# Sums of squares on TensorE between the products, behind four norms of a two-block network

## The reference

```python
def rmsnorm(x, g):
    y = xf * lax.rsqrt(jnp.mean(xf * xf, axis=-1, keepdims=True) + NORM_EPS)
    return (y * g.astype(jnp.float32)).astype(x.dtype)
# first block, for layer i
    a = rmsnorm(h, norm_mix_pre[i])
    m = mla_mixer(a, ...) if i % 2 == 0 else pool_mixer(a, ...)
    h = h + rmsnorm(m, norm_mix_post[i])
    f = conv_ffn(rmsnorm(h, norm_ffn_pre[i]), ...)
    h = h + rmsnorm(f, norm_ffn_post[i])
# second block
    u = _rmsnorm(h, ln1_g[i]); proj = u @ w_in[i]
```

## Time and profile before

| | |
|---|---|
| median of 3 runs | 948.71 us (945.36 to 949.46) |
| profiled execution | 950.01 us, span 948.2 us |
| mean granted TensorE clock | 0.984 |
| busy: TensorE, VectorE, ScalarE, GpSimd | 96%, 72%, 54%, 29% |
| first products of f0, a1, f1, g start at | 142.7, 354.5, 387.7, 592.2 us |

### The profile page before, as it was taken

The page is one execution under the profiler, slowest core; times in us unless marked ns, Lnnn a source line. Parts: engine busy times, 40 slices in busy tenths (PEclk is TensorE's granted clock), DMA queues, the critical chain, the costliest instruction groups (busy, mean ns, idle before and its releaser), DMA issues.

```text
span 948.2 us, 19994 instructions
## 1 busy us (share of the span) xinstructions
PE 912.0 (96%) x7354; PEld 884.7 (93%) x7354; DVE 681.7 (72%) x1168; ACT 512.9 (54%) x851; POOL 276.4 (29%) x202
## 2 busy tenths in 40 slices
PE   6999999999999999999999999999989999999996
PEld 6986798999999997899999999999989999999995
DVE  7767529999994225699999533889777888785666
ACT  5765656666655346566666544454455554454443
POOL 4118752000015534200000464200024334345633
PEclk9999999999999998799999999999999999999997
DMA  7541132544554531144445554354234555465431
GB/s 249 181 158 46 46 134 89 178 177 177 177 196 164 210 133 46 45 177 177 177 177 210 184 188 174 96 194 157 89 113 174 185 201 182 177 227 184 166 134 45
DMA packets 22147, 146.80 MB, mean 155 GB/s; under 512 B 2752, under 2 KB 5328, under 8 KB 6736
## 3 DMA queue, kind: packets, MB, share of 16 engines
q1 hardware_dynamic: 22096, 146.11, 43.1%
HBM read 143.94 MB, written 1.05 MB: 153 GB/s over the span
## 4 chain that ended last, share of the span: by engine, by line
PE 83%; DVE 10%; ACT 3%; issue 2%; POOL 1%; DMA 0%; POOLq 0%; SPq 0%; DVEq 0%; ACTq 0%
PE bank L441 23%; PE bank L442 23%; PE bank L443 23%; PE bank L681 2%; DVE u_low L1332 2%; ACT w_high L959 1%; DVE w_low L1323 1%; PE bank L529 1%; DVE h L1405 1%; PE bank L814 1%; DVE bank L1397 1%; PE bank L697 1%; PE bank L543 1%; PE bank L715 1%; PE bank L512 1%
## 5 line engine op out<-in xcount | busy, mean ns | idle before, releaser
L441 PE MATMUL bank<-u_high,w_high 128*128 128x256 f32 (+2 forms) x1400 | 401.7, 287 | 13.1 <-DVE u_low L1332 8.6
L442 PE MATMUL bank<-u_low,w_high 128*128 128x256 f32 (+2 forms) x1400 | 399.4, 285 | 0.0
L443 PE MATMUL bank<-u_high,w_low 128*128 128x256 f32 (+2 forms) x1400 | 398.2, 284 | 0.0
L1832 POOL TENSOR_TENSOR w_low<-raw,w_high 128x512 fp32r<-128x512 f32 (+1 forms) x60 | 168.8, 2814 | 463.0 <-ACT w_high L959 463.0
L1323 DVE TENSOR_TENSOR w_low<-raw,w_high 128x1024 fp32r<-128x1024 f32 (+5 forms) x119 | 198.1, 1664 | 125.7 <-ACT w_high L959 124.6
L441 PEld LDWEIGHTS bank<-u_high,w_high 128*128 128x128 f32 x1400 | 266.1, 190 | 15.5 <-DVE u_low L1332 8.1
L442 PEld LDWEIGHTS bank<-u_low,w_high 128*128 128x128 f32 x1400 | 265.8, 190 | 0.0
L443 PEld LDWEIGHTS bank<-u_high,w_low 128*128 128x128 f32 x1400 | 265.5, 190 | 0.0
L959 ACT ACTIVATE w_high<-raw 128x1024 fp32r<-128x1024 f32 (+5 forms) x119 | 195.2, 1640 | 73.2 <-PE bank L443 65.0
L441 PE MATMUL bank<-x_high,w_high 128*128 128x256 f32 (+1 forms) x608 | 173.9, 286 | 4.4 <-ACT x_high L1261 2.5
L443 PE MATMUL bank<-x_high,w_low 128*128 128x256 f32 (+1 forms) x608 | 173.3, 285 | 0.0
(11 more groups left out here) (213 smaller groups left out, 1030.1 us busy)
## 6 DMA issues: line engine op xcount, KB each, us to landing
raw<-w_up_dram SPq DMA_DIRECT2D x66, 1024.0 KB, 4.8
raw<-w_down_dram SPq DMA_DIRECT2D x24, 1408.0 KB, 6.1
raw<-w_gin_c_dram SPq DMA_DIRECT2D x4, 1536.0 KB, 6.8
raw<-w_wo_dram SPq DMA_DIRECT2D x4, 1024.0 KB, 5.0
raw<-w_wout_dram SPq DMA_DIRECT2D x4, 1024.0 KB, 4.9
raw<-w_pgate_dram SPq DMA_DIRECT2D x4, 1024.0 KB, 4.7
raw<-w_gin_v_dram SPq DMA_DIRECT2D x2, 1024.0 KB, 4.7
raw<-w_gin_g_dram SPq DMA_DIRECT2D x2, 1024.0 KB, 6.2
```

The lines of the kernel that those rows point to most:

```text
L441: nc.tensor.matmul(out, hi, rhi, start=start, stop=False)
L442: nc.tensor.matmul(out, hi, rlo, start=False, stop=False)
L443: return nc.tensor.matmul(out, lo, rhi, start=False, stop=stop)
L1832: nc.gpsimd.tensor_tensor(wl[n % 2][:, at], raw[n % 2][:, at], wh[n % 2][:, at].bitcast(F32), ALU.subtract).then_inc(low_parts_g, pool_cou ...
```

## The change

- In the first unit of f0, f1 and g TensorE takes the sums of chunk k - 1 over m between chunk k's products with u_high and those with u_low; behind the unit only chunk 7's sums are left. The eps product moves to the first of these.
- In a1 the sums of chunks 0 to 2 stand between the first tile's products of the first half, those of 3 to 7 in a row between the halves.
- GpSimd no longer adds squares or clears `acc` for these four norms.
- In `add_post` (all four places) the scaled chunk is written back to m, and the addition reads it there.

```diff
@@ unit
+                        if sums is not None and k > 0:
+                            sums(k - 1)
                         low_ready(k)
...
+            def sums_by_chunks(name, n):
+                def of(k):
+                    if k == 0:
+                        nc.tensor.matmul(bank[NORM_BANK][:, 0:n], eps_w[:, :], ones[:, 0:n], start=True, stop=False,
+                                         skip_group_check=True)
+                    chunk_sums(name, n, k)
+                return of
...
@@ ffn_up
-                unit(n0, T, us, high_then_low(sums_name))
-                norm_sums(sums_name, f"{sums_name} acc {DC - 2}", squares(0, T), True)
+                n = len(squares(0, T))
+                if l < 2:
+                    unit(n0, T, us, high_then_low(sums_name), sums=sums_by_chunks(sums_name, n))
+                    last_sums(sums_name, n)
+                else:
+                    unit(n0, T, us, high_then_low(sums_name))
+                    norm_sums(sums_name, f"{sums_name} acc {DC - 2}", squares(0, T), True)
...
@@ a1
+                                if half == 0 and 2 * g + k > 0:
+                                    sums(2 * g + k - 1)
                                 low_ready(2 * g + k)
...
                 if half == 0:
-                    norm_sums("a1", f"a1 acc {DC - 2}", squares(0, T1), True)
+                    for k in range(DC // 2 - 1, DC - 1):
+                        sums(k)
+                    last_sums("a1", len(TT))
...
@@ g
-            unit(n, T, us, high_then_low("g"))
-            norm_sums("g", f"g acc {DC - 2}", squares(0, T), True)
+            unit(n, T, us, high_then_low("g"), sums=sums_by_chunks("g", len(squares(0, T))))
+            last_sums("g", len(squares(0, T)))
...
@@ add_post
-                spare = 3 * (unit % 2) + 2
-                normed = bank[NORM_BANK][:, 64:64 + Tm], bank[spare][:, 0:Tm]
...
-                    nc.vector.tensor_tensor(normed[c % 2], m[:, c, 0:Tm], bank[R_BANK][:, 0:Tm], ALU.mult)\
+                    nc.vector.tensor_tensor(m[:, c, 0:Tm], m[:, c, 0:Tm], bank[R_BANK][:, 0:Tm], ALU.mult)\
...
-                        nc.vector.tensor_tensor(h[:, c, T1 - Tm:T1], h[:, c, T1 - Tm:T1], normed[c % 2], ALU.add)\
+                        nc.vector.tensor_tensor(h[:, c, T1 - Tm:T1], h[:, c, T1 - Tm:T1], m[:, c, 0:Tm], ALU.add)\
...
@@ add_square on GpSimd
-                if name in SQUARES_IN_M:
-                    pool.wait_ge(*done(f"{name} u low {c}"))
...
@@ GpSimd, the same for a1, f1 and g
-            for c in range(DC - 1):
-                add_square("f0", c, T1, done(f"f0 sq {c}"))
             up_lows(0)
-            clear("f0")
```

More of the change, by code:

```diff
@@ L446, in weights, with unit @@
                 return wh[n % 2][:, j * P:(j + 1) * P], wl[n % 2][:, j * P:(j + 1) * P]
-            def unit(n, T, xs, chunk_ready=None, middle=None, i=None, order=None, first_low=None, between={}):
+            def unit(n, T, xs, chunk_ready=None, middle=None, i=None, order=None, first_low=None, between={}, sums=None):
                 U = UNITS[n]
@@ L785, in _ @@
             parts_ready(n)
+            sums = sums_by_chunks("a1", len(TT))
             for half in range(2):
@@ L1892, in _ @@
             clear("post0")
-            for c in range(DC - 1):
-                add_square("f0", c, T1, done(f"f0 sq {c}"))
             up_lows(0)
-            clear("f0")
             down(0, T1)
             clear("fpost0")
-            for c in range(DC - 1):
-                add_square("a1", c, T1, done(f"a1 sq {c}"))
-            clear("a1")
             for b in range(DC - 2):
@@ L1905, in _ @@
             clear("post1")
-            for c in range(DC - 1):
-                add_square("f1", c, SEQ + HISTORY, done(f"f1 sq {c}"))
             up_lows(1)
-            clear("f1")
             down(1, SEQ)
@@ L1912, in _ @@
             clear("fpost1")
-            for c in range(DC - 1):
-                add_square("g", c, T, done(f"g sq {c}"))
             for n in range(FIRST_UNIT["gin_a"] + 2, FIRST_UNIT["gin_c"] + 6):
                 low(n)
-            clear("g")
             for u in range(4):
```

## The result

The changed kernel takes 952.74 us (median of 20 executions, 948.74 to 959.76) against 949.19 us of the kernel before beside it (20 executions, 944.39 to 952.36): ratio 1.0037, 95% interval 1.0022 to 1.0052. It is a little slower, by about 0.4%. The prediction was 952.9 us. The profiled execution took 953.30 us, its span is 951.5 us.

A forecast was written before the change was run, and what follows sets the result against it. TensorE was taken to bound the kernel, VectorE to pace f0's first unit. 0.56 + 0.90 + 0.93 + 1.78 - 1.7 + 1.7 = +4.2 us, from the runs' median 948.71 us to 952.9 us; range 948.5 to 959.0 us.

The forecast's parts named there:

- each chunk's sums cost 0.67 us: First units of f0, f1, g: 0.67 us of sums (g 0.45) exceed the 0.41 us wait, so TensorE becomes the bound.
- The term for it without cover: VectorE's longer addition from m: at most 2.2 us over four norms if TensorE's 0.22 us surplus per chunk didn't hide it.
- The low part of the next unit: VectorE, behind f0's first unit: ends at about 153.7 instead of 154.3 us, so TensorE's wait for it goes.
- Its own term, +1.78 us: a1: chunks 3 to 7's sums in a row, 3.35 us, replace 1.57 us of eps and sums between the halves.
- I count one more such stretch: +1.7 us: a1: the row of sums brings one more low-clock stretch, sized like the one behind f1, +1.7 us.
- 3.35 us with nothing but one-column sums: a1: reason given for the added low clock; the row is longer than the tail that cost f1 its clock.
- I count -1.7 us: Behind f1: the new tail has no wait and one chunk of sums, so the low clock there goes, -1.7 us.
- rival (c): Clock gives more back: f0's and f1's tails fall often before, never after, a1 loses none; +0.8 us, 949.5 us, chance 0.11.
- (a): Clock falls inside the first units: 954.6 to 960 us in f0 or f1 alone, up to 967 in both; chance 0.28.
- (b): Sums hide in the waits if a chunk's six passes take at most 0.41 us: -3.3 us, 945.4 us; chance 0.07.
- (d): A later wait absorbs the delay of the sums: +0, 948.7 us; chance 0.04.
- The chance of 0.44: Whole kernel slower by over 0.5% (above 953.5 us): 0.17 from the main forecast plus 0.27 from (a).

The follow-up runs named there:

- e6: The changed kernel without the sums of chunks 0 to 6 in f0, f1 and g (left out altogether): 947.45 us against 947.95, ratio 0.9991.
- e2: The kernel before with only the scaled block written to m, all sums still on GpSimd: 949.58 us against 948.49, ratio 1.0021.
- e1: The changed kernel with the scaled block going to PSUM again, so only the sums move to TensorE: 953.27 us against 948.49, ratio 1.0050.
- e4: The changed kernel with squares written as fp32r into x_high and summed in one pass instead of two: 939.78 us against 948.49, ratio 0.9928.
- e3: The changed kernel with a1's sums on GpSimd and over acc again: 949.15 us against 948.49, ratio 1.0025.
- e8: The changed kernel with f0, f1 and g back on GpSimd, only a1 with the new sums: 953.93 us against 947.95, ratio 1.0063.
- e5: The changed kernel with a1's sums of chunks 3 to 6 spread between second and third token tile's products: 954.62 us against 947.95, ratio 1.0060.
- e7: The one-pass kernel e4 with a1's sums of chunks 3 to 6 spread as in e5: 942.59 us against 947.95, ratio 0.9927.
- e10: The one-pass kernel e4 with 32 equal columns for each sum instead of 2: 943.53 us against 948.35, ratio 0.9955.
- e11: The changed kernel without a1's sums of chunks 0 to 6 (left out altogether): 947.18 us against 948.35, ratio 1.0000.
- e12: The one-pass kernel e4 measured once more, unedited, against the kernel before: 942.77 us against 948.02, ratio 0.9939.
- e9: The changed kernel with each sum of f0, a1, f1 and g written to 32 equal columns: 952.26 us against 948.35, ratio 1.0033.

## Why the prediction was right

**What bounds the first units.** Right, to the hundredth. The chunk was worked out as 0.75 + 0.67 = 1.42 us and is 1.42 us; e6 shows that without the passes it is 1.11 us. f0: +0.59 measured, +0.56 predicted. f1: +0.82 against +0.90. g: +1.00 against +0.93. In g's six later chunks the step from sums to sums is 1.51 us, predicted 1.50. The step "each chunk's sums cost 0.67 us" (0.45 in g) held.

**VectorE.** Right that the move to m would be hidden. The term for it without cover (at most 2.2 us) had the right size by luck: e2, without cover, pays 2.1 us, hardly by a longer addition (0.35 us in a steady chunk) but by a u_low that takes 0.59 us beside GpSimd, and the accumulation 0.85. It came out at nothing for the reason that GpSimd has left, and not only by TensorE's surplus: VectorE's chunk is 1.11 us with the block in PSUM (e1) and with the block in m, and in e4 it is so where VectorE sets the pace again. The low part of the next unit was predicted to end at 153.7 us; it ends at 152.65, since it takes 2.28 us and not 2.85 without GpSimd's last accumulation beside its start. The step took its length from the earlier trace rows unchanged. It had no effect, since TensorE's sums end later.

**a1.** Its own term, +1.78 us, held, and two more were off. By the loads, the first half without its last row takes 10.36 us (354.58 to 364.94; before 354.50 to 364.52, 10.02): +0.34 us for eps and the sums of chunks 0 to 2, which the working put at nothing without saying so. The row takes 3.99 us (364.94 to 368.93) and the second half 6.46 us (368.93 to 375.39), where they took 1.57 and 4.20. Thirty passes are 3.35 us at full clock, 1.78 more than 1.57; so the low clock took 0.64 us of the row and 2.26 us of the second half. The step "I count one more such stretch: +1.7 us" was mis-sized: 2.9 us, since the stretch runs on through the second half's products. The experiments give 1.5 us (e3 against the changed kernel) and 1.6 us (e8 against e2, roughly) for own work.

The step's reason was incomplete as well: "3.35 us with nothing but one-column sums" is not needed for it. e5 loses 8.5 us with twelve passes in a row, and its clock is low before them. What the runs have in common is the passes: in the profiled executions a1 has a low clock worth 5.1 to 8.5 us with fp32 sums of one column in its first half (changed, e1, e5, e6, e8), 1.7 to 3.4 us with GpSimd's sums, none, or one pass (before, e2, e3, e4, e7, e10, e11, e12), and nothing with 32 columns (e9). In e9 the loads and the waits are the same as in the changed kernel and the clock is not; that is one profiled execution, one of three such in nine. Over all executions the column is 12.8 to 16.3 us in the five kernels and 8.8 to 12.7 us in the nine, but e3 (12.5) and the kernel before (12.7) are hardly below the changed kernel (12.8). So that these passes hold the clock down in a1 is likely from the traces, and not shown.

**f1's tail.** "In the changed kernel that tail has no wait [...] I count -1.7 us" held in size: from f1's end to g's start the changed kernel is 1.56 us shorter. The old tail of sums and wait lost its clock in four of six places that were profiled (f0 and f1 in the kernel before, e2 and e8: f1; f0; both), the new one in none of 22 (f0 and f1 in eleven kernels). Which of the old tails falls looks like chance. Half of rival (c) held so far: old tails fall in most of the places, new ones in none. Its other half, that a1 loses none, didn't. But "has no wait" is not the reason: in e4 TensorE waits in f0's tail from about 151.65 us, when the last passes end, to 152.74 us, longer than the 0.63 us of before, and keeps its clock. What went is the row of eps, acc and last chunk, 14 passes of which 12 send one column; whether that is the reason wasn't tested.

**What was left out.** post1's norm ahead of f1 gave 1.3 us back. That it did so in the one execution is the trace's word; over the executions the column is 12.8 us after and 12.7 before. So the clock terms cancel as predicted, but by +2.9 - 1.6 - 1.3 and not by +1.7 - 1.7, and that is luck: one term was too small, and one wasn't there. That the forecast of 952.9 us came within 0.2 us of the median owes something to it. Why post1's stretch was shorter wasn't tested: e8 has the long one there and e5 the short one, both with a1's new sums, so it may be chance.

**The rivals.** (a) The clock didn't fall inside f0's, f1's or g's first unit in any profiled kernel; in the kernel before and in seven others a stretch that began in post1's norm still reached f1's first products, in the changed kernel it ended 0.4 us ahead of them. Windows of f0 in the changed kernel:

```profile
146.00:148.00 2.00, 2.00 (x20) 1.93 (x19) 2.00 (x7) 1.67 (x4) 0.00 (x0) 1.00 0.04 8
```

(b) The passes are not short: the six loads of a chunk take 0.68 us (145.72 to 146.40), the two of the narrow tile included. The Trainium skill (TensorE: Matmul & The Clock Gate, LDWEIGHTS) would make the two 16-wide ones nearly free; the trace disagrees, with 0.112 us per pass for all six. The 16-wide load by itself is shorter, 0.09 us against 0.19, but three tiles take 0.67 to 0.68 us and g's two full ones 0.45. e4 shows what (b) would have brought had they been half as long. (d) Nothing absorbed the delay. The chance of 0.44 for slower by over 0.5% was high: 0.37% was measured, though the interval ends at 0.52%.

## What to carry to other kernels

Before giving an idle engine's work to the one that holds the path, put the time of its passes beside the wait that they are to fill: 0.67 us into 0.41 us costs, and 0.33 us into the 0.36 us that VectorE's shorter chunk leaves (1.11 - 0.75) is free. What counts here is the number of passes and not the arithmetic: the same sums with the squares in fp32r, in half the passes, turned a loss of 0.4% into a gain of 0.6 to 0.7%. And where single executions differ by the granted clock, split each time by its clock before reading a difference of a few microseconds, and trust the split most where the clocks are alike.

## What was not expected of the hardware

A place in SBUF instead of PSUM costs VectorE nothing by itself and 0.09 us per chunk while GpSimd works beside it (e2). VectorE's low part of 128 x 2048 takes 2.28 us with GpSimd idle and 2.85 us with one accumulation of 0.91 us beside its start, of which some 0.7 us overlap: 0.57 us lost, most of the overlap, where a u_low lost 0.10 us of an overlap of 0.29 (148.10 to 148.39 in the kernel before). The Trainium skill (SBUF — State Buffer, Who interferes with whom) has such a pair exclude each other for the whole instruction; the low part's row comes near to that, the u_low's does not. TensorE, busy without a gap in the profile, ran at 1.2 GHz from 360 to 374 us in e5, with one column behind many of its loads; in the profiled execution of e9, with 32 columns behind each such load, it kept 2.4 GHz through a1. At the low clock six one-column passes took 1.11 us against 0.67, and so less than double.
